# RWKV on one Trainium2 core: the last four steps of the chain of states set among the k tiles of a gate block

## The reference, cut to what matters

```python
def step(state, inp):
    r_t, w_t, k_t, v_t, a_t, b_t = inp
    sa = jnp.einsum('bhvk,bhk->bhv', state, a_t)
    state = (state * w_t[:, :, None, :] + sa[..., None] * b_t[:, :, None, :]
             + v_t[..., None] * k_t[:, :, None, :])
    return state, jnp.einsum('bhvk,bhk->bhv', state, r_t)
...
mean = jnp.mean(y, -1, keepdims=True)
var = jnp.mean(jnp.square(y - mean), -1, keepdims=True)
y = ((y - mean) * lax.rsqrt(var + RW_LN_EPS)).reshape(B, S, RW_WIDTH) * ln_w + ln_b
```

## Time and profile before

| | |
|---|---|
| median of 3 runs | 2814.61 us |
| the profiled execution's own time | 2815.15 us |
| its span in the profile | 2813.3 us |
| TensorE busy | 2744.0 us, 98% of the span |
| VectorE, ScalarE, GpSimd busy | 1631.2, 955.9, 944.7 us |
| chain that ended last | 92% TensorE |
| granted TensorE clock, mean | 0.999 |

### The profile page before, as it was taken

One profiled execution on the slowest core, in us unless ns is written; L12 is line 12 of the kernel. 1 busy time (PEld: TensorE's weight loads), 2 busy tenths in 40 slices (PEclk: granted clock), 3 DMA queues, 4 the chain that ended last, 5 costly groups with the idle time before them and its releaser, 6 DMA issues.

```text
span 2813.3 us, 60969 instructions
## 1 busy us (share of the span) xinstructions
PE 2744.0 (98%) x25491; PEld 2289.8 (81%) x25491; DVE 1631.2 (58%) x1807; ACT 955.9 (34%) x1447; POOL 944.7 (34%) x691
## 2 busy tenths in 40 slices
PE   5999999999999999999999999999999999999999
PEld 4797989798989898988787777788887788888887
DVE  4645454545454545469694667466648543333896
ACT  5312121212121212135455768301113333333443
POOL 0403030303030303034343111233333477777443
PEclk9999999999999999999999999999999999999999
DMA  5202020202020202033332111356511133234353
GB/s 210 75 21 60 22 60 21 61 21 61 21 61 21 61 21 61 11 116 115 122 110 71 37 58 50 123 192 216 170 57 53 45 113 108 83 105 141 125 168 94
DMA packets 255360, 235.00 MB, mean 84 GB/s; under 512 B 24354, under 2 KB 213884, under 8 KB 255100
## 3 DMA queue, kind: packets, MB, share of 16 engines
q1 hardware_dynamic: 241632, 183.74, 21.6%
q10 hardware_dynamic: 13467, 47.31, 4.7%
HBM read 184.08 MB, written 46.92 MB: 82 GB/s over the span
## 4 chain that ended last, share of the span: by engine, by line
PE 92%; DVE 3%; ACT 2%; issue 1%; DMA 0%; SPq 0%; POOL 0%; ACTq 0%; DVEq 0%; POOLq 0%
PE ps L306 68%; PE ps L1241 3%; PE ps L1255 3%; PE ps L1252 2%; PE ps L1219 2%; PE ps L1304 1%; PE ps L1441 1%; PE ps L1466 1%; PE ps L1209 1%; PE ps L1454 1%; PE ps L1175 1%; PE ps L1288 1%; PE ps L1261 1%; PE ps L1307 1%; PE ps L1157 1%
## 5 line engine op out<-in xcount | busy, mean ns | idle before, releaser
L306 PE MATMUL ps<-x_hi,w_hi 128*128 128x512 f32 (+1 forms) x2372 | 801.5, 398 | 6.4 <-DVE x_lo L2854 2.4
L306 PE MATMUL ps<-x_lo,w_hi 128*128 128x512 f32 (+1 forms) x2372 | 783.1, 390 | 0.0
L306 PE MATMUL ps<-x_hi,w_lo 128*128 128x512 f32 (+1 forms) x2372 | 783.1, 390 | 0.0
L296 POOL CAST w_hi<-w_raw 128x1024 fp32r<-128x1024 f32 (+2 forms) x161 | 154.0, 957 | 1545.4 <-PE ps L306 1290.7
L306 PEld LDWEIGHTS ps<-x_hi,w_hi 128*128 128x128 f32 (+1 forms) x2372 | 436.9, 187 | 114.8 <-issue 21.7
L306 PEld LDWEIGHTS ps<-x_hi,w_lo 128*128 128x128 f32 (+1 forms) x2372 | 444.0, 187 | 96.7
L306 PEld LDWEIGHTS ps<-x_lo,w_hi 128*128 128x128 f32 (+1 forms) x2372 | 444.2, 187 | 92.7
L298 POOL TENSOR_TENSOR w_lo<-w_raw,w_hi 128x1024 fp32r<-128x1024 f32 (+2 forms) x161 | 330.1, 2050 | 12.9
L306 PE MATMUL ps<-x_sums,w_hi 128*128 128x512 f32 x648 | 201.8, 392 | 0.6 <-issue 0.6
L1052 POOL TENSOR_TENSOR w_lo<-arena,w_hi 128x384 fp32r<-128x384 f32 (+1 forms) x124 | 155.7, 1256 | 109.4 <-ACT w_hi L2211 109.4
L2514 DVE COPY_PREDICATED arena<-hid,ps 128x256 f32<-128x256 int32 x144 | 71.9, 499 | 141.7 <-PE ps L1252 90.0
(11 more groups left out here) (346 smaller groups left out, 4374.5 us busy)
## 6 DMA issues: line engine op xcount, KB each, us to landing
w_raw<-in_w_in SPq DMA_DIRECT2D x78, 512.0 KB, 4.0
arena<-in_w_ada SPq DMA_DIRECT2D x48, 512.0 KB, 6.1
arena<-gates_sig ACTq DMA_DIRECT2D x40, 512.0 KB, 4.3
w_raw<-in_w_ffn_in SPq DMA_DIRECT2D x26, 512.0 KB, 4.2
gates_sig<-arena ACTq DMA_DIRECT2D x24, 512.0 KB, 2.7
under<-in_w_ffn_in SPq DMA_DIRECT2D x18, 512.0 KB, 5.8
hidden_sums<-arena SPq DMA_DIRECT2D x36, 256.0 KB, 2.6
under<-hidden_sums SPq DMA_DIRECT2D x11, 768.0 KB, 6.5
```

Source lines behind the costliest of these rows:

```text
L296: nc.gpsimd.tensor_copy(hi, raw).then_inc(s_whi, 1)
L306: ins = nc.tensor.matmul(dst[h], wp, xp[h], start=first and m == 0, stop=last and m == 2, skip_group_check=on)
```

## The change

The body of the loop over the steps becomes a function `state_step(c)`. Steps 1 to 11 are written in a row as before. Steps 12, 13, 14 and 15 are written by the hook of block 5: behind its k tile 0 comes step 12, behind tile 1 step 13, behind tile 2 step 14, behind tile 3 step 15. Tiles 4 to 7 follow without steps between them. TensorE's program alone is changed; VectorE, ScalarE, GpSimd and SyncE have the same programs, and every instruction and every wait of TensorE is still there.

```diff
                 y_own(0)
                 y_own(1)
-                for c in range(1, CHUNKS):
+                def state_step(c):
+
                     if c > 1:
                         pe.wait_ge(v_s, upto(i * STEPS + c - 1))
                         wait_alone(pe)
...
                     if c + 1 < CHUNKS:
                         y_own(c + 1)
-                dense(pe, Block("rwkv", 5, i))
+                for c in range(1, CHUNKS - 4):
+                    state_step(c)
+
+                def last_steps(k):
+
+                    if k < 4:
+                        state_step(CHUNKS - 4 + k)
+                dense(pe, Block("rwkv", 5, i), after=last_steps)
                 pe.wait_ge(v_post, upto(i * POST + 5))
                 for j in range(T // P):
                     ins = pe.transpose(ps[:, 4 + j // 4, j % 4 * P:(j % 4 + 1) * P], rw["A"][:, j * P:(j + 1) * P], ident)
```

## The result

The changed kernel takes 2833.16 us (median of 4 runs, 2831.0 to 2834.82); the kernel before took 2814.64 us beside it. The ratio is 1.0061 [1.0049, 1.0073]: 18.5 us slower, where 15.3 were forecast and 2824 to 2839 us was the range. The profiled execution has 2834.82 us and a span of 2833.0 us.

A forecast was written before the change was run, and what follows sets the result against it. TensorE was taken to bound the kernel. Per turn, 0.38 us of switching and 1.53 us of new stall made +1.91 us, +15.3 us over 8 turns, giving 2829.9 us; the 8-in-10 range was 2824 to 2839 us.

The forecast's parts named there:

- The bound: Whole kernel: TensorE, busy 98% of the span and 92% of the chain, decides; time changes only where it starts earlier or later.
- Part 1: Before steps 12 to 15: TensorE's waits on VectorE, 0.34 us a step, go, covered by more than 1.3 us of tile.
- Part 2: Steps among tiles: switching between small and large matmuls makes a step with its tile 2.18 us; 0.38 us a turn.
- Part 3: Before step 12: first tile puts it at 210.70 against 209.02; the L1288 pause stays at full length, 3.9 us in 8 times.
- Part 4: Behind step 15: 5.85 us of TensorE work no longer covers the 7.38 us chain; transposes stall 1.53 us a turn.
- Nothing given back: Rest of the turn: no later wait of TensorE takes up the loss, so all +15.3 us reaches the end.
- A: Scaling behind step 15: GpSimd's cast begins first and delays it, another 1.08 us a turn; 2838.5 us; 15%.
- B: Products before step 12: the L1288 pause goes, 0.70 us a turn less loss, the rest as forecast; 2824.3 us; 10%.
- C: Steps 12 to 15: switching costs nothing and the pause goes too; -0.27 us a turn, 2812.4 us, no change; 4%.
- D: Steps 12 to 15: switching is free but the pause stays; +0.48 us a turn, 2818.5 us; 5%.
- E: Steps 12 to 15: switching is dearer, 0.80 us a step instead of 0.60; 0.6 us a turn more, 2834.7 us; 8%.

The follow-up runs named there:

- experiment 1: Changed kernel with only steps 14 and 15 moved, behind tiles 0 and 1, six tiles left behind step 15; 2813.92 us against 2813.82 for the kernel before.
- experiment 7: Changed kernel with steps 10 to 15 behind tiles 0 to 5 and the transposes behind tile 3 of the next block; 2816.51 us against 2815.33 before.
- experiment 3: Kernel before with all 64 key-square matmuls behind tile 3 instead of 16 behind each of tiles 0 to 3; 2811.54 us against 2813.82.
- experiment 5: Kernel before with the key squares in two groups of 32, behind tiles 1 and 3; 2807.80 us against 2815.33.
- experiment 6: Changed kernel with the moved steps in pairs: 12 and 13 behind tile 0, 14 and 15 behind tile 1; 2815.83 us against 2815.33 before.
- experiment 8: Kernel before with one gate-block tile set before step 11, steps 11 to 15 in a row behind it, then seven tiles; 2811.20 us against 2816.06.
- Experiment 2: Changed kernel with the eight transposes issued behind tile 1 of the next block instead of in front of it; 2815.86 us against 2813.82 before.
- experiment 4: Changed kernel with one more VectorE operation of 0.17 us, and the wait for it, ahead of the scaling; 2843.37 us against 2813.82 before.

## Why the prediction was right

The mechanism came as forecast, and the time is 3.2 us over the likeliest one (18.5 for 15.3). 1.95 us of that are in the stretch; they are a sum of misses of both signs (+1.3 the pause, +0.8 in the first steps, +0.5 for steps of 2.20 instead of 2.18, -0.7 behind step 15). That the total came so near is in part luck.

- **The bound.** TensorE ends everything; the count of instructions is the same and the loss is its idle time. Right.
- **Part 1, the waits on VectorE go.** Right: steps 12 to 15 start without a bracket in the timeline.
- **Part 2, switching.** The 2.18 us for a step and its tile, taken from the key squares in the same trace, was measured at 2.19 to 2.21 in the changed kernel and at 2.20 in experiments 1 and 7. A price read from matmuls of another width (one column for 64) held, with the 0.04 us that the prediction added: a group of state products takes 0.61 us up to the next tile (210.31 to 210.92), a group of key squares 0.56. A pair of switches is 0.30 to 0.33 us by experiments 3 and 5, and for a state step it is 2.20 - 1.36 - 0.46 = 0.38 us by the same estimate; it eats the 0.34 of waiting that it fills; experiment 6 shows the same from the other side.
- **Part 3, the first tile and the pause.** This is the term that was mis-sized. I kept the pause at its full length (3.9 us of idle time); it was 5.2, longest 0.9 instead of 0.6. In the first turn the last products start at 208.41 where 0.59 us of idle stood before them. In six other kernels that still have it the sum is 4.1 to 5.0, so it differs from one execution to the next by as much as the error. It makes 1.3 of the 1.95 us by which the stretch is over the forecast; the second pause at step 4, which I had not seen, makes 0.6. My argument that it belongs to its place was half right: it stayed here, but experiments 7 and 8 make it go by a tile set before it. Counting the records of TensorE (matmuls, weight loads and waits) from the start of step 1, the pause at L1288 begins behind the 363rd to 365th record in all 64 turns of the eight kernels that have it. In 14 of these turns the smaller pause is plain to see too, and it stands exactly 256 records earlier every time. The Trainium skill (Advanced Engine Details and Errata, section ISA Cache) gives the instruction cache lines of 256 instructions, and this distance agrees with it. That a late fetch is the cause has still not been shown; no record shows a fetch. In experiment 8 the place 256 records behind the smaller pause is nine records into step 11, right behind the tile, and TensorE doesn't stop there. So the place says where the pause can come, and a tile before it takes it away.
- **Part 4, the new stall.** 1.44 us by the starts against 1.53, in all 8 turns; as idle time 1.30 us and 10.3 in all, against 12; 7.29 from step 15 to the transposes against 7.38. Experiment 2 shows that with this wait nearly the whole loss goes (+2.0 instead of +18.5 us), and experiment 1 that it isn't there with two steps.
- **Nothing given back.** Right: the rest of the turns moved by -0.8 us, within what the pauses before step 1 do between profiles. One thing outside was not foreseen: 3.4 us by a clock fall in a later stage, behind a wait of 0.97 us. The wait alone doesn't bring it: the profiles of experiments 2 and 6 have it too (0.97 and 0.96 us), with no fall there. Experiments 1 and 8 have the fall and no loss of time, so nothing ties it to the change. It isn't in all runs of the changed kernel alike: the profiled one has a mean clock of 0.998, the other three 0.999. How much of the 3 us between 18.5 and 15.3 it holds stays open.
- **The rivals.** A did not come, by the margin forecast (0.16 us against 0.17), and experiment 4 shows that it was real. B was wrong for this change and right for a tile placed before step 11. C and D needed free switching, E dearer; both are excluded by 2.19.

## What to carry to other kernels

Before work is moved out of a stretch that covers a chain on other engines, measure that chain and the cover: here 7.4 us under 11.3, so two tiles (2.7 us) could be taken and four (5.4) could not, and the remedy was to give the consumer something else to do first. Filling a short wait with another kind of matmul is paid for in switches; read the price from a place in the same trace where both kinds alternate, and look for longer rows of one kind instead (32 instead of 16: 4.85 us by the traces, 7.5 by the medians). And between two engines that contend, a fifth of a microsecond decides who waits.

## What the runs showed of the hardware

- A pair of changes between 128x512 tiles and groups of small fp32 matmuls costs TensorE 0.30 to 0.33 us over the time of the group (experiments 3 and 5, one column). With 64 columns a group of 16 takes 0.05 us more up to the next tile (0.61 for 0.56).
- The granted clock can fall under an engine that is busy all the time: behind 64 one-column matmuls in a row (2.0 us) it did in 3 of 8 turns, to 0.76 over the 7 us behind, and behind 32 (1.0 us) in none. Behind the 2.3-us stalls of experiment 4 it fell in 3 of 8 turns, behind the 1.3-us stalls of the changed kernel in none of the eight. Which of the eight turns is hit, no run here explains.
- VectorE and GpSimd with operands in SBUF share badly but in order: the one that begins first keeps its time (1.22 or 1.04 us), the other one ends about 0.9 us late (1.97 for 1.04, 2.08 for 1.22).
- A pause of 0.3 to 1.1 us of TensorE in a row of some hundred small matmuls stands at the same instruction in every turn, 256 of TensorE's records behind a smaller one of 0.2 us, and goes when one large tile stands before it (experiments 7 and 8). The cause is only argued: something that has to keep up with the pace of instructions.
